# x loaded in three parts and normed as it arrives, and the set-up of vectors and bias table placed among the first projections, in a four-layer fp32 block on one core

## The reference

```python
def rmsnorm(x, g):
    xf = x.astype(jnp.float32)
    y = xf * lax.rsqrt(jnp.mean(xf * xf, axis=-1, keepdims=True) + EPS)
    return (y * g.astype(jnp.float32)).astype(x.dtype)
...
u = rmsnorm(x, norm_pre[i])
...
q, kc, vc, ks, vs, kw, vw, gate, z = jnp.split(u @ w_in, points, axis=-1)
...
bias_w = jnp.transpose(table_g[rel_bucket(dist_w)], (2, 3, 0, 1))
```

## Time and profile before

| | us |
|---|---|
| median of 3 runs | 2272.48 (2271.74, 2272.48, 2279.61) |
| the profiled execution, whole | 2274.92 |
| its span | 2273.0 |
| first transpose of `Norm` starts | 23.82 |
| first product of `NsaProject` starts | 39.64 |
| bias matmuls start, next product starts | 106.47, 114.97 |

### The profile page before, as it was taken

The page is one execution under the profiler, slowest core; times in us unless marked ns, Lnnn a source line. Parts: engine busy times, 40 slices in busy tenths (PEclk is TensorE's granted clock), DMA queues, the critical chain, the costliest instruction groups (busy, mean ns, idle before and its releaser), DMA issues.

```text
span 2273.0 us, 33586 instructions
## 1 busy us (share of the span) xinstructions
PE 2070.1 (91%) x13582; PEld 1661.5 (73%) x13582; DVE 848.5 (37%) x1813; ACT 935.9 (41%) x1707; POOL 915.2 (40%) x636
## 2 busy tenths in 40 slices
PE   4999999999997968997588899999999899999998
PEld 3889756788765746776477588888878568888886
DVE  2100467340027375146565353333033524334301
ACT  3431477453247354443133353444143535344422
POOL 2431267534446322341012734455434542544542
PEclk9987999999998969898589999999999999999999
DMA  4322100123310211221210323333322121333332
GB/s 119 93 78 65 47 20 2 48 69 101 93 56 19 70 42 49 76 75 38 49 31 19 101 62 98 102 93 111 102 75 84 38 66 56 102 97 98 103 111 74
DMA packets 222361, 161.05 MB, mean 71 GB/s; under 512 B 30631, under 2 KB 205295, under 8 KB 222208
## 3 DMA queue, kind: packets, MB, share of 16 engines
q1 hardware_dynamic: 220016, 151.83, 22.6%
q0 software_dynamic: 2192, 7.07, 1.0%
HBM read 153.64 MB, written 5.24 MB: 70 GB/s over the span
## 4 chain that ended last, share of the span: by engine, by line
PE 79%; DVE 9%; ACT 4%; POOL 3%; issue 3%; DMA 1%; POOLq 1%; SPq 0%; DVEq 0%; PEld 0%; PEldq 0%; ACTq 0%
PE ps L386 15%; PE ps L348 13%; PE ps L350 13%; PE ps L359 13%; PE ps L396 7%; PE ps L1355 2%; PE ps L1368 2%; PE ps L1344 2%; POOL weights_lo L289 1%; DVE ps L901 1%; DVE buffer L906 1%; PE ps L1082 1%; PE ps L2892 1%; PE ps L2156 1%; PE ps L1703 1%
## 5 line engine op out<-in xcount | busy, mean ns | idle before, releaser
L289 POOL TENSOR_TENSOR weights_lo<-buffer,weights_hi 128x1024 fp32r<-128x1024 f32 (+1 forms) x265 | 654.0, 2470 | 981.4 <-ACT weights_hi L278 981.2
L278 ACT ACTIVATE weights_hi<-buffer 128x1024 fp32r<-128x1024 f32 (+1 forms) x265 | 276.4, 1045 | 340.7 <-PE ps L396 285.5
L348 PE MATMUL ps<-u_hi,weights_hi 128*128 128x512 f32 (+1 forms) x752 | 278.5, 378 | 5.6 <-DVE u_lo L681 3.0
L350 PE MATMUL ps<-u_lo,weights_hi 128*128 128x512 f32 (+1 forms) x736 | 274.8, 377 | 0.0
L1931 ACT ACTIVATE buffer<-ps,buffer 128x512 f32<-128x512 f32 x88 | 68.7, 781 | 276.4 <-PE ps L359 276.4
L359 PE MATMUL ps<-u_hi,weights_lo 128*128 128x512 f32 (+1 forms) x752 | 177.2, 378 | 0.0
L1961 DVE SCALAR_TENSOR_TENSOR buffer<-ps,buffer,buffer 128x511 f32<-128x511 f32 x88 | 66.0, 750 | 287.7 <-ACT buffer L1931 287.7
L348 PEld LDWEIGHTS ps<-u_hi,weights_hi 128*128 128x128 f32 x752 | 141.2, 190 | 32.0 <-issue 5.6
L350 PEld LDWEIGHTS ps<-u_lo,weights_hi 128*128 128x128 f32 x736 | 138.4, 188 | 25.5
L359 PEld LDWEIGHTS ps<-u_hi,weights_lo 128*128 128x128 f32 x752 | 137.0, 191 | 25.8
L2932 ACT ACTIVATE buffer<-ps 32x256 f32<-32x256 f32 (+5 forms) x96 | 47.7, 498 | 152.9 <-PE ps L2892 68.1
(11 more groups left out here) (403 smaller groups left out, 4277.5 us busy)
## 6 DMA issues: line engine op xcount, KB each, us to landing
buffer<-in_w_up SPq DMA_DIRECT2D x88, 512.0 KB, 3.8
buffer<-in_w_down SPq DMA_DIRECT2D x44, 512.0 KB, 3.4
buffer<-in_diff_w_in SPq DMA_DIRECT2D x32, 512.0 KB, 4.0
buffer<-in_nsa_w_in SPq DMA_DIRECT2D x28, 512.0 KB, 3.8
buffer<-in_w_rkv SPq DMA_DIRECT2D x24, 512.0 KB, 4.1
buffer<-in_nsa_w_out SPq DMA_DIRECT2D x8, 512.0 KB, 3.5
buffer<-in_diff_w_out SPq DMA_DIRECT2D x8, 512.0 KB, 3.6
buffer<-in_w_o_rwkv SPq DMA_DIRECT2D x8, 512.0 KB, 3.4
```

The costliest lines, as they stand in the source:

```text
L278: self.nc.scalar.activation(self.part_hi[:, part % self.PARTS, 0:n], self.raw[:, ld % self.RAW, 0:n], ACT.Copy).then_inc(self.hi_ready, 1)
L289: self.nc.gpsimd.tensor_tensor(self.part_lo[:, part % self.PARTS, 0:n], self.raw[:, ld % self.RAW, 0:n], self.part_hi[:, part % self.PARTS ...
L348: nc.tensor.matmul(out, hi[:, k, :], rhs[0][:, k, tokens], start=(k == 0), stop=False)
L350: nc.tensor.matmul(out, hi[:, k, :], rhs[1][:, k, tokens], start=False, stop=False)
```

## The change

`x` comes in three DMAs: tile 0, tile 1, and tiles 2 and 3, each with a semaphore of its own; the constants' DMA stands behind the first. The first three weight loads follow, and only then the bias table, the one-hot table and the vectors (`load_vectors`). `Setup` and `Norm` let all four engines go on, so no engine waits for the others ahead of the first product. ScalarE begins with a root of `eps`, which loads its function table, and waits for each tile's own part of `x`; its multiplication `unit` is gone, and VectorE does both multiplications in one instruction (`scale`, a scalar_tensor_tensor) after its reciprocal. The transposes of the vectors, their copies and the table's preparation go to `NsaProject`: on TensorE behind the 12 groups and ahead of the bias matmuls, on VectorE ahead of the bias copies. The vectors go through banks 6 and 7, so the third and later bias sets wait for their copies. `rows`, `tab` and `tab_rest` lie elsewhere. In `FfnUp` both layers share five semaphores and count on from each other; what each instruction waits for is the same there, and the hunks of that class are left out but for the first.

```diff
@@ -503,17 +503,19 @@
 class Setup(Stage):
 
 
+
     def __init__(self, env):
         super().__init__(env)
         self.bias = env.take(HEADS, T, at=env.words - HEADS * T)
-        at = env.area
+        at = env.area + KD * T + 2 * GROUPS * T
         self.rows = env.take(6, P, at=at)
-        self.tab = env.take(HEADS, at=at + 1000)
-        self.tab_rest = env.take(HEADS, at=at + 1016)
+        self.tab = env.take(HEADS, at=at + 6 * P)
+        self.tab_rest = env.take(HEADS, at=at + 6 * P + HEADS)
+        self.tensor_goes_on = self.scalar_goes_on = self.vector_goes_on = self.gpsimd_goes_on = True
         self.hot = env.hot = env.ctx.enter_context(env.nc.sbuf_tensor("one_hot", [P, NDIST], BF16))
         self.tab_hi = env.ctx.enter_context(env.nc.sbuf_tensor("table_parts", [P, 3, HEADS], BF16))
         self.table3 = env.ctx.enter_context(env.nc.sbuf_tensor("table3", [P, HEADS], BF16))
-        self.x_arrived = env.sem("x_arrived")
+        self.x_arrived = [env.sem(f"x_arrived{i}") for i in range(3)]
         self.table_ready = env.sem("table_ready")
         self.rows_zeroed = env.sem("rows_zeroed")
         self.bias_ready = env.sem("bias_ready")
@@ -525,8 +527,14 @@
 
     def load(self, sp):
         env, io, nc = self.env, self.env.io, self.env.nc
-        sp.dma_start(env.x, io["x"].rearrange("b (t p) d -> p (b t) d", p=P)).then_inc(self.x_arrived, 16)
-        sp.dma_start(env.const, io["shape_constants"]).then_inc(self.const_arrived, 16)
+        for i, end in enumerate((1, 2, NT)):
+            sp.dma_start(env.x[:, i:end, :],
+                         io["x"][0, i * P:end * P, :].rearrange("(t p) d -> p t d", p=P)).then_inc(self.x_arrived[i], 16)
+            if i == 0:
+                sp.dma_start(env.const, io["shape_constants"]).then_inc(self.const_arrived, 16)
+
+    def load_vectors(self, sp):
+        io = self.env.io
         sp.wait_ge(self.rows_zeroed, 1)
         for part in range(3):
             sp.dma_start(self.tab[32 * part:32 * part + 32, :], io["rel_bias_table"]).then_inc(self.tab_arrived, 16)
@@ -549,23 +557,23 @@
             put(3 + 2 * l, 44, 44, vec(io["conv_b_2"][l]))
     N_ROWS = 3 + 4 + 3 + 6
 
-    def tensor(self, pe):
+    def vectors_tensor(self, pe):
         env, nc = self.env, self.env.nc
         pe.wait_ge(self.rows_arrived, 16 * self.N_ROWS)
-        pe.wait_ge(self.const_arrived, 16)
-        pe.wait_ge(self.tab_arrived, 64)
         for n in range(6):
             size = [128, 56, 88, 88, 88, 88][n]
-            tr = nc.tensor.transpose(env.ps[:, n // 4, (n % 4) * P:(n % 4) * P + size], self.rows[0:size, n, :],
+            tr = nc.tensor.transpose(env.ps[:, 6 + n // 4, (n % 4) * P:(n % 4) * P + size], self.rows[0:size, n, :],
                                      env.ident[0:size, 0:size])
         tr.then_inc(self.vec_ready, 1)
 
     def bias_tensor(self, pe):
 
         env, nc = self.env, self.env.nc
+        pe.wait_ge(self.tab_arrived, 64)
+        pe.wait_ge(self.table_ready, 1)
         for i in range(8):
-            if i >= 4:
-                pe.wait_ge(self.bias_taken, i - 3)
+            if i >= 2:
+                pe.wait_ge(self.bias_taken, max(i - 2, 1))
             for c in range(32):
                 at = DIST0 + P - c - 32 * i
                 mm = nc.tensor.matmul(env.ps[:, 4 + i % 4, c * HEADS:(c + 1) * HEADS], self.hot[:, at:at + P],
@@ -573,12 +581,14 @@
             mm.then_inc(self.bias_ready, 1)
 
     def vector(self, dve, step):
-        env, nc = self.env, self.env.nc
-        nc.vector.memset(env.eps, EPS)
+        nc = self.env.nc
+        nc.vector.memset(self.env.eps, EPS)
         nc.vector.memset(self.tab[:], 0.0).then_inc(self.rows_zeroed, 1)
+
+    def table_vector(self, dve, step):
+        nc = self.env.nc
         dve.wait_ge(self.tab_arrived, 64)
         dve.wait_ge(self.rows_zeroed, 1)
-
         step(nc.vector.tensor_copy(self.tab_hi[:, 0, :], self.tab))
         step(nc.vector.tensor_tensor(self.tab_rest, self.tab, self.tab_hi[:, 0, :], ALU.subtract))
         step(nc.vector.tensor_copy(self.tab_hi[:, 1, :], self.tab_rest))
@@ -588,12 +598,16 @@
             q = slice(32 * part, 32 * part + 32)
             nc.vector.tensor_copy(self.table3[q, :], self.tab_hi[q, part, :])
         nc.vector.memset(self.table3[96:128, :], NEG).then_inc(self.table_ready, 1)
+
+    def vectors_vector(self, dve, step):
+        env, nc = self.env, self.env.nc
         dve.wait_ge(self.vec_ready, 1)
         o = 0
         for n in range(6):
             size = [128, 56, 88, 88, 88, 88][n]
-            step(nc.vector.tensor_copy(env.vec[:, o:o + size], env.ps[:, n // 4, (n % 4) * P:(n % 4) * P + size]))
+            cp = nc.vector.tensor_copy(env.vec[:, o:o + size], env.ps[:, 6 + n // 4, (n % 4) * P:(n % 4) * P + size])
             o += size
+        cp.then_inc(self.bias_taken, 1)
 
     def bias_vector(self, dve, step):
         env, nc = self.env, self.env.nc
@@ -643,6 +657,14 @@
             dve.wait_ge(env.next_g_arrived, 16 * self.g_n)
             nc.vector.tensor_tensor(self.un[:, i, :], env.x[:, i, :], env.next_g, ALU.mult)
 
+    def scale(self, dve, i):
+
+        env, nc = self.env, self.env.nc
+        dve.wait_ge(env.next_g_arrived, 16 * self.g_n)
+        dve.wait_ge(env.rstd_ready, self.n + i + 1)
+        nc.vector.scalar_tensor_tensor(self.un[:, i, :], env.x[:, i, :], self.rstd[:, i:i + 1], env.next_g,
+                                       ALU.mult, ALU.mult).then_inc(env.un_ready, 1)
+
     def invert(self, dve, i):
 
         dve.wait_ge(self.env.rms_ready, self.n + i + 1)
@@ -694,31 +716,44 @@
 class Norm(Stage):
 
 
-    def __init__(self, env, g_row, u, x_arrived):
+    def __init__(self, env, g_row, u, setup):
         super().__init__(env)
-        self.norm, self.x_arrived = Renorm(env, g_row, u), x_arrived
+        self.norm, self.setup = Renorm(env, g_row, u), setup
+        self.tensor_goes_on = self.scalar_goes_on = self.vector_goes_on = self.gpsimd_goes_on = True
 
     def gpsimd(self, pool, step):
         self.norm.fetch(pool)
         self.env.split_lo(pool, 1)
 
     def scalar(self, act, step):
-        act.wait_ge(self.x_arrived, 16)
-        for i in range(NT):
-            self.norm.square(act, step, i)
-            self.norm.unit(act, i)
-        self.env.split_hi(act, 1)
-        for i in range(NT):
-            self.norm.high(act, i)
+        env, norm = self.env, self.norm
+        act.wait_ge(self.setup.rows_zeroed, 1)
+        env.nc.scalar.activation(env.sqrt_junk, env.eps, ACT.Sqrt)
+
+        def square(i):
+            act.wait_ge(self.setup.x_arrived[min(i, 2)], 16)
+            norm.square(act, step, i)
+
+        for i in range(3):
+            square(i)
+        norm.high(act, 0)
+        square(3)
+        norm.high(act, 1)
+        env.split_hi(act, 0)
+        norm.high(act, 2)
+        norm.high(act, 3)
+        env.split_hi(act, 1)
 
     def vector(self, dve, step):
         for i in range(NT):
-            self.norm.gain(dve, i)
             self.norm.invert(dve, i)
-        for i in range(NT):
-            self.norm.low(dve, i)
+            self.norm.scale(dve, i)
+            if i:
+                self.norm.low(dve, i - 1)
+        self.norm.low(dve, NT - 1)
 
     def tensor(self, pe):
+        pe.wait_ge(self.setup.const_arrived, 16)
         for i in range(NT):
             self.norm.turn(pe, i)
         self.norm.wait(pe)
@@ -953,9 +988,10 @@
         u = self.m.u
         for ld, g in self.q + self.kvc:
             project_features(env, pe, ld, u, g)
+        self.setup.vectors_tensor(pe)
         self.setup.bias_tensor(pe)
 
-        pe.wait_ge(self.setup.bias_taken, 8)
+        pe.wait_ge(self.setup.bias_taken, 9)
         for keys, (lds, g) in self.branches:
             for ld, gk in keys:
                 project_features(env, pe, ld, u, gk)
@@ -964,6 +1000,8 @@
         project_tokens(env, pe, [ld], u, g)
 
     def vector(self, dve, step):
+        self.setup.table_vector(dve, step)
+        self.setup.vectors_vector(dve, step)
         self.setup.bias_vector(dve, step)
 
     def gpsimd(self, pool, step):
@@ -1880,18 +1918,15 @@
         for j in range(FT):
             for half in range(2):
                 self.lds += [ld for ld, _ in load_features(env, w, half * D_FF + j * P, P)]
-        n = str(layer)
-        self.scaled, self.scaled_before = m.scaled, 2 * FT * layer
-        self.gelu_done, self.gelus_before = m.gelu_done, FT * layer
-        self.product_ready = env.sem("product_ready" + n)
-        self.act_hi_ready, self.act_done = env.sem("act_hi_ready" + n), env.sem("act_done" + n)
+        self.scaled, self.gelu_done, self.product_ready, self.act_hi_ready, self.act_done = m.signals
+        self.tiles_before = FT * layer
         self.tensor_goes_on = True
 
     def wait_banks_free(self, pe):
         pe.wait_ge(self.env.proj_taken, self.g0 + 2 * FT)
 
     def wait_result(self, pe, k):
-        pe.wait_ge(self.act_done, k + 1)
```

(15 more changed lines are left out.)

4 lines of the change are left out of this document (2 added, 2 removed).

## The result

| | us |
|---|---|
| changed kernel, median of 7 runs (range) | 2263.76 (2258.68 to 2268.75) |
| kernel before, median of 7 runs | 2275.24 (2271.74 to 2280.05) |
| ratio, with 95% interval | 0.9941 (0.9922 to 0.9961) |
| profiled execution, whole and span | 2268.75, 2266.6 |
| first product starts | 24.72 (before 39.64) |

The kernel became 0.6% faster, which is the forecast in per cent; in microseconds it is 11.5 by the medians, where 14.3 were forecast. The time of 2263.76 lies 0.24 us inside the upper end of the range.

A forecast was written before the change was run, and what follows sets the result against it. TensorE was taken as the bound, standing still before the first product and at the bias. 16.1 us gained at the start less 1.8 lost at the bias gave 14.3, so 2272.48 becomes 2258.2 us, range 2254 to 2264.

The forecast's parts named there:

- The bound and what goes: Ahead of the first product: TensorE stands behind vector DMAs, meetings and the late row; without them 16.1 us gained.
- When the data lands: Loads at the start: row and x tile 0 share evenly, landing at 6.1; tile 1 at 8.25, tiles 2 and 3 at 10.9.
- The norm, step by step: Walk from first square to first product: last remainder ends at 23.3, first product starts at 23.5 instead of 39.64.
- The bias grows: Between group 12 and the bias: the moved transposes (1.2) and copies (1.5) lose 1.8 us (1.1 to 2.3).
- The clock: TensorE's half-speed stretches at the first product and behind the bias: no change, +-1.5 us for each place.
- The sum: Whole kernel: 16.1 - 1.8 = 14.3 us gained, median from 2272.48 to 2258.2, 0.6% less.
- The late row: Rival at the norm: row lands near 11.5, first product at 26.1, gain 11.7, time 2260.8; chance 0.17.
- The clock that comes up at once: Rival at the first product: x isn't slowed and no slow stretch; gain 17.0, time 2255.5; chance 0.12.
- The clock that stays down over groups: Rival in the first projections: 4.8 us more per group; chance 0.04 that all is lost, 0.07 more for a part.
- The change that does nothing by its parts: Rival at the norm: first copy waits for x's third part anyway, so early tiles gain little; no chance given.

The follow-up runs named there:

- row_early: Kernel before with one edit: GpSimd doesn't wait at the end of the set-up, so the norm's row loads at the start; ratio 0.9997 (0.9987 to 1.0006).
- split_late: Changed kernel with ScalarE's split of the first weight behind the copy of tile 2 instead of ahead of it; first product 1.37 us earlier.
- x_whole: Changed kernel with x in one DMA again, the constants behind it; ratio to the kernel before 0.9955 (0.9939 to 0.9970).

## Why the prediction was right, point by point

- **The bound and what goes.** Right. The first product moved by 14.9 us, because the wait for the vectors, the row behind it and the meetings are gone: 6.4 us by the earlier start of the norm, 2.8 by the row, 3.0 by the parts of x, 2.7 by the rest. With the row alone early, and the vectors still ahead of the norm, only 1.3 us came (`row_early`).
- **When the data lands.** The end was right for the step that counts (third part 10.9, measured 11.15), the way there was not. I let the row and tile 0 share evenly and land at 6.1 each. Tile 0 came at 4.28, as if alone, and the row at 8.32, 6.9 us after its issue, longer than any of the five in rows 5. The row paid for the sharing, not tile 0. It cost nothing, since the first copy waits for the third root anyway.
- **The norm, step by step.** Right in its order throughout; 23.5 forecast, 24.72 and 25.25 measured. The mis-sized term is the multiplication of tile 3: 1.29 from a row of line 901, whose operand lies in PSUM; with both operands in SBUF and GpSimd's split beside it, 2.71. I had walked GpSimd's split (15.9 to 19.3) and VectorE's multiplication (17.4 to 18.9) through the same microseconds and asked only whether one needs the other's data. `split_late` gives back 1.37 us, more than the 1.2 by which 24.72 missed.
- **The bias grows.** Right in kind, too large: 1.8 forecast, 0.82 measured. The transposes took 0.77 us in the chain where I had 1.2, the copies 1.03 where I had 1.5: both shrank more than I gave for a running engine and for copies without a wait between them. With 0.82 the loss lies below my lower bound of 1.1.
- **The clock.** The first slow stretch did not stay as it was: by the chain, matmuls took 0.43 us until 28.5 in the first profile (3.8 us), 30.7 in the second (5.5) and 28.8 in the third (4.2), against 2.9 before. Behind the bias it lasted 5.9 us instead of 6.3. At 0.20 us lost in each 0.43, that is 0.4 to 1.2 us of time at the start and 0.2 back behind the bias, within the +-1.5 that I kept. What I did not put into the sum is the scatter of some 10 us behind split 18, in either kernel, which was there to be seen in the spread of the three runs (2271.74 to 2279.61).
- **The sum.** 14.3 forecast at the place behind the bias, 13.76 measured there. Two errors, -1.2 for the norm and +1.0 for the bias, nearly cancel, and that is luck. The other 0.3 is the longer slow stretch at the start: the way from the first product to the end of the groups took 67.17 us instead of 66.83. At the end of the program the gain is smaller than the sum: 11.5 by the times (pooled: 10.1 by medians, 11.9 by means). The sum took it that all of the 14.3 arrives there; some 2 us do not, and the cause is open. The agreement in per cent is in part luck too: in the series of the result the kernel before came out at 2275.24, 2.8 us over the 2272.48 from which the forecast starts.
- **The rivals.** The late row: it was late, by 2.2 us, not by 5.4, and moved nothing. The clock that comes up at once: not so, it took longer than before. The clock that stays down over groups: not so; from 40 to 96 the granted clock was 1.00. The change that does nothing by its parts: refuted by `x_whole`, 3.0 us.

## What to carry to other kernels

When a start is laid out on paper, look at each pair of instructions of VectorE and GpSimd that fall into the same microseconds, and not only at who needs whose data: here one such pair cost 1.4 us on the path, and moving the one that nobody waits for gave it back. On an engine that holds the path, do first what feeds another engine (the multiplication that TensorE waits for) and afterwards what is only needed at the end; that one exchange gave 3.4 us, 1.4 of them since the multiplication also left GpSimd's way. And before a gain of 0.5% is read from the end of two profiles, compare them at a place up to which two executions of the same kernel agree (here split 18, to 0.6 us), and see how far apart these two are at the end.

## What the runs showed that I had not expected

- The same program, on the same instructions, took some 9.5 us more or less from one execution to the next, most of it in stretches with long phases of half clock: across the programs 66.4 to 71.3 us between splits 18 and 24, 264.9 to 271.4 between splits 104 and 108.
- Two loads of 512 KB, issued 0.6 us apart on two queues, did not share evenly: tile 0, issued first, landed by 4.28, the row by 8.32.
- A 128x16 copy of 0.17 us took 1.95 us beside a 128x1024 instruction of GpSimd.
- During 256 matmuls of 16 columns in a row, which started at 92.65, the granted clock fell to half at 96.8 and was still there when the long matmuls went on (0.58 over 102 to 108); with the same in eight portions between groups of long matmuls it was not (1.00 from 45 to 130).
